# Adding returned rows and last products before gating, and a reordered beginning of the expert stage

## The reference, cut to what matters

```python
for gi in range(N_GROUPS_2):
    hg = jnp.einsum('td,edf->tef', xf, w_gate[gi])
    hu = jnp.einsum('td,edf->tef', xf, w_up[gi])
    act = jax.nn.silu(hg) * hu * comb[:, gi, :, None]   # comb: 0 for experts a token does not use
    out = out + jnp.einsum('tef,efd->td', act, w_down[gi])
...
h = h + gate_f * _hierarchical_moe(xf, ...)
return _rms_norm(h, norm_out_w)
```

## Time and profile before

| | |
|---|---|
| three runs | 1900.52, 1903.16, 1905.74 us, median 1903.16 |
| the profiled execution | 1896.68 us, its span 1894.8 us |
| TensorE busy | 1846.8 us (97%) |
| VectorE busy | 1221.7 us (64%) |
| ScalarE busy | 943.2 us (50%) |
| POOL busy | 104.2 us (5%) |
| mean granted TensorE clock | 0.99 |

### The profile page before, as it was taken

How to read it: one execution, slowest core, us unless ns; L and a number is a source line. 1 busy time by engine, 2 the same in 40 slices (tenths; PEclk the granted TensorE clock), 3 DMA queues, 4 the chain that set the end, 5 groups by cost and what they waited for, 6 DMA issues and landing times.

```text
span 1894.8 us, 24459 instructions
## 1 busy us (share of the span) xinstructions
PE 1846.8 (97%) x9398; PEld 1525.2 (80%) x9398; DVE 1221.7 (64%) x1319; ACT 943.2 (50%) x1035; POOL 104.2 (5%) x118
## 2 busy tenths in 40 slices
PE   8999999999999999999999999989999989999997
PEld 6888998888888888888888888878888778876764
DVE  5566766566654566655555666787645767868677
ACT  5434535444544464544435443564445446767574
POOL 0100000000000000000100000103100050000000
PEclk8999999999999999999999999999999999999999
DMA  6877465777455556554746776535233357979794
GB/s 231 291 254 245 144 200 177 245 249 245 155 194 187 189 169 203 178 178 146 93 80 190 253 250 215 165 116 173 90 112 134 112 213 239 329 248 339 250 336 185
DMA packets 239273, 379.16 MB, mean 200 GB/s; under 512 B 13511, under 2 KB 149069, under 8 KB 239184
## 3 DMA queue, kind: packets, MB, share of 16 engines
q1 hardware_dynamic: 233728, 365.13, 57.3%
q0 software_dynamic: 5456, 12.81, 4.0%
HBM read 372.83 MB, written 10.30 MB: 202 GB/s over the span
## 4 chain that ended last, share of the span: by engine, by line
PE 91%; DVE 5%; ACT 2%; DMA 1%; issue 1%; SPq 0%; POOLq 0%; ACTq 0%; DVEq 0%
PE ps L373 26%; PE ps L375 26%; PE ps L374 26%; PE ps L1056 2%; PE ps L1078 1%; DVE lo L356 1%; PE ps L2756 1%; PE ps L760 1%; PE ps L1066 1%; ACT hi L350 1%; PE ps L1545 1%; PE ps L1034 1%; DVE late L1913 1%; PE ps L1560 0%; PE ps L487 0%
## 5 line engine op out<-in xcount | busy, mean ns | idle before, releaser
L356 DVE TENSOR_TENSOR lo<-raw,hi 128x2048 fp32r<-128x2048 f32 x296 | 678.1, 2296 | 326.2 <-ACT hi L350 325.0
L350 ACT ACTIVATE hi<-raw 128x2048 fp32r<-128x2048 f32 x296 | 565.2, 1915 | 364.5 <-PE ps L375 355.2
L373 PE MATMUL ps<-hi,xT_hi 128*128 128x512 f32 x1376 | 549.8, 400 | 14.4 <-DVE lo L356 7.9
L375 PE MATMUL ps<-hi,xT_lo 128*128 128x512 f32 x1376 | 538.3, 391 | 0.0
L374 PE MATMUL ps<-lo,xT_hi 128*128 128x512 f32 x1376 | 538.1, 391 | 0.0
L373 PEld LDWEIGHTS ps<-hi,xT_hi 128*128 128x128 f32 x1376 | 259.6, 189 | 69.7 <-issue 9.8
L375 PEld LDWEIGHTS ps<-hi,xT_lo 128*128 128x128 f32 x1376 | 259.4, 189 | 56.0
L374 PEld LDWEIGHTS ps<-lo,xT_hi 128*128 128x128 f32 x1376 | 260.0, 189 | 49.6
L373 PE MATMUL ps<-hi,ffn_hhi 128*128 128x512 f32 x352 | 137.8, 391 | 0.0
L375 PE MATMUL ps<-hi,ffn_hlo 128*128 128x512 f32 x352 | 137.1, 389 | 0.0
L374 PE MATMUL ps<-lo,ffn_hhi 128*128 128x512 f32 x352 | 137.0, 389 | 0.0
(11 more groups left out here) (449 smaller groups left out, 2225.5 us busy)
## 6 DMA issues: line engine op xcount, KB each, us to landing
raw<-in_ffn_w_in SPq DMA_DIRECT2D x176, 512.0 KB, 4.6
raw<-in_ffn_w_out SPq DMA_DIRECT2D x88, 512.0 KB, 4.1
raw<-in_attn_w_qkv SPq DMA_DIRECT2D x72, 512.0 KB, 4.6
raw<-in_w_in SPq DMA_DIRECT2D x64, 512.0 KB, 4.4
modraw<-in_mod_w SPq DMA_DIRECT2D x48, 512.0 KB, 6.5
raw<-in_w_gate SPq DMA_DIRECT2D x48, 512.0 KB, 4.5
raw<-in_w_up SPq DMA_DIRECT2D x48, 512.0 KB, 5.8
raw<-in_w_down SPq DMA_DIRECT2D x48, 512.0 KB, 4.4
```

What stands on the lines that cost most here:

```text
L350: nc.scalar.activation(hi[u % SPLIT][:, :], raw[raw_slot(u)][:, :], ACT.Copy).then_inc(S("hi_ready"), 1)
L356: nc.vector.tensor_tensor(lo[u % SPLIT][:, :], raw[raw_slot(u)][:, :], hi[u % SPLIT][:, :].bitcast(F32), ALU.subtract).then_inc(S("lo_read ...
L373: nc.tensor.matmul(dst, w_hi, x_hi, start=start, stop=False, skip_group_check=True)
L375: return nc.tensor.matmul(dst, w_lo, x_hi, start=False, stop=stop, skip_group_check=True)
```

## The change

1. *The end:* both returned rows of both tiles are added first; then, per tile, the products are added out of PSUM, the whole is gated once and added to `h`. `add_gated` for this stage is gone.
2. *The first silus:* the silu table is loaded by a one-column activation after the router's exponentials. A new semaphore `gu_first` is counted when block 0 (block 2) is finished, halfway through the last gate/up unit of position 0 (1), and the first silu waits for that. silu(0) and gate_up(0) come ahead of the gathers of batch 0. Each unit of position 1 waits only for its own pair of gathers.
3. *Routing values:* `info(1)` makes position 1's blocks only, at the old place; the others follow after position 2's second, third and fourth unit. VectorE takes the first part where it took all, and the rest ahead of `inner_lo(3)`; the down units of position 1, and POOL's scatter, wait for the rest.
4. *inner_hi(2) and inner_lo(2)* move ahead of the rounding and the split of position 2's last unit.

```diff
+                           ("weight_rest", 1), ("dest_rest", 1)),
...
-            pool.wait_ge(S("dest_ready"), AT["dest_ready"] + 1)
+            pool.wait_ge(S("dest_rest"), AT["dest_rest"] + 1)
...
             nc.scalar.activation(R("se", 4), R("sx", 4), ACT.Exp).then_inc(S("rt_exp"), 1)
+            nc.scalar.activation(root[:, :], eps[:, :], ACT.Silu)
             round_unit(act, u0 + 3)
...
                 for b in blocks or BLOCKS[n]:
-                    wait_used(act, GUU[n] + 3)
+                    if n < 2 and b == BLOCKS[n][0]:
+                        act.wait_ge(S("gu_first"), n + 1)
+                    else:
+                        wait_used(act, GUU[n] + 3)
...
+            silu(0, 0)
+            silu(0, 1)
             gathered(0, 0)
             gathered(0, 2)
             gathered(0, 4)
             gathered(0, 6)
-            silu(0, 0)
-            silu(0, 1)
             round_unit(act, GUU[1] + 1)
...
+                    if n == 2 and i == 3:
+                        inner_hi(2)
                     round_unit(act, u)
...
-                    if n == 2 and i == 3:
-                        inner_hi(2)
...
-                        dve.wait_ge(S("weight_ready"), AT["weight_ready"] + 1)
+                        ready = "weight_ready" if n == 1 else "weight_rest"
+                        dve.wait_ge(S(ready), AT[ready] + 1)
...
+            def block_info(mm, bs, weight_sem, dest_sem):
+
+                dve.wait_ge(S(mm), AT[mm] + 1)
+                info = ps[:, 5, 0:4 * N_ROUTED].rearrange("p (b q) -> p b q", q=4)[:, bs, :]
+                then(nc.vector.tensor_copy(winfo[:, bs], info[:, :, 3:4].rearrange("p b q -> p (b q)")))
+                nc.vector.tensor_tensor(weight[:, bs], winfo[:, bs], info[:, :, 2:3].rearrange("p b q -> p (b q)"),
+                                        ALU.add).then_inc(S(weight_sem), 1)
+                then(nc.vector.tensor_scalar(dinfo[:, bs], info[:, :, 1:2].rearrange("p b q -> p (b q)"), 1.0, moe_cols[:, 20:21],
+                                             ALU.subtract, ALU.mult))
+                nc.vector.tensor_tensor(dest[:, bs], dinfo[:, bs], info[:, :, 0:1].rearrange("p b q -> p (b q)"),
+                                        ALU.add).then_inc(S(dest_sem), 1)
+
             split_unit(dve, GUU[1])
+            gate_up(0, 0)
+            gate_up(0, 1)
             gathered(0, 1)
             gathered(0, 3)
             gathered(0, 5)
             gathered(0, 7)
-            gate_up(0, 0)
-            gate_up(0, 1)
             split_unit(dve, GUU[1] + 1)
...
+                        block_info("info_mm", slice(0, 2), "weight_ready", "dest_ready")
                         gate_up(1)
...
+                    if n == 2 and i == 3:
+                        inner_lo(2)
                     split_unit(dve, u)
...
-                    if n == 2 and i == 3:
-                        inner_lo(2)
...
                         split_unit(dve, u)
                         if n == 2 and i == 0:
+                            block_info("info_rest", slice(2, N_ROUTED), "weight_rest", "dest_rest")
                             inner_lo(3)
...
             for t in range(TT):
                 dve.wait_ge(S(f"y_loaded{t}"), 32)
-                then(nc.vector.tensor_tensor(y_back[:, t, 0, :], y_back[:, t, 0, :], y_back[:, t, 1, :], ALU.add))
+                nc.vector.tensor_tensor(y_back[:, t, 0, :], y_back[:, t, 0, :], y_back[:, t, 1, :], ALU.add).then_inc(S("y_summed"), 1)
+            for t in range(TT):
+                dve.wait_ge(S("y_summed"), t + 1)
+                wait_acc(dve, DNU[0][1], t)
+                for c in range(2):
+                    y = y_back[:, t, 0, c * 512:c * 512 + 512]
+                    nc.vector.tensor_tensor(y, y, ps[:, 2 * t + c, :], ALU.add).then_inc(S("gated"), 1)
+                dve.wait_ge(S("gated"), 4 + 2 * t + 2)
                 then(nc.vector.tensor_tensor(y_back[:, t, 0, :], y_back[:, t, 0, :], gate_row[:, 1, :], ALU.mult))
-                then(nc.vector.tensor_tensor(h[:, t, :], h[:, t, :], y_back[:, t, 0, :], ALU.add))
+                nc.vector.tensor_tensor(h[:, t, :], h[:, t, :], y_back[:, t, 0, :], ALU.add).then_inc(S("h_ready"), 2)
...
                     pe.wait_ge(S("picked"), 2 * IN_BATCH[m][-1])
+                if m == 1 and f == 0:
+                    pe.wait_ge(S("fill_hi"), 4)
+                    pe.wait_ge(S("fill_lo"), 4)
...
-                    if i == 0:
+                    if n == 1:
+                        pe.wait_ge(S("fill_hi"), i + 1)
+                        pe.wait_ge(S("fill_lo"), i + 1)
+                    elif i == 0:
...
+                    if n < 2 and i == 3 and j == 1:
+                        last.then_inc(S("gu_first"), 1)
...
                     pe.wait_ge(S("e_lo"), BLOCKS[n][-1] + 1)
+                    if n == 1:
+                        pe.wait_ge(S("dest_rest"), AT["dest_rest"] + 1)
...
-            def info():
+            def info(*experts):
...
-                pe.wait_ge(S("picked"), 2 * (N_POS - 1))
-                for n in range(1, N_POS):
+                pe.wait_ge(S("picked"), 2 * experts[-1])
+                if experts[0] > 1:
+                    pe.wait_ge(S("dest_ready"), AT["dest_ready"] + 1)
+                for n in experts:
...
             gate_up_unit(1, 2)
-            info()
+            info(1)
             gate_up_unit(1, 3)
...
                         turn(2 + i)
+                    if n == 2 and i:
+                        info(*((2, 3, 4, 5), (6, 7, 8, 9, 10), range(11, N_POS))[i - 1])
...
-            add_gated(dve, DNU[0][1], 1, ysb_all, 1, (0, 1, 2, 3))
```

More of the change, by code:

```diff
@@ L105, in build @@
             "moe_vector": (("rt_gx", 1), ("rt_sx", 1), ("chosen", 2), ("order_ready", 1), ("rank_read", 1), ("slot_ready", 2), ("xtok_lo", 4),
-                           ("info_vals", 4), ("weight_ready", 1), ("dest_ready", 1)),
+                           ("info_vals", 4), ("weight_ready", 1), ("dest_ready", 1),
+                           ("weight_rest", 1), ("dest_rest", 1)),
             "moe_scalar": (("rt_exp", 2), ("xtok_hi", 4), ("back_ready", 1), ("last_hi", 2)),
-            "moe_tensor": (("rt_mm", 1), ("rank_mm", 1), ("x_turned", 2), ("info_mm", 1), ("last_turned", 1)),
+            "moe_tensor": (("rt_mm", 1), ("rank_mm", 1), ("x_turned", 2), ("info_mm", 1), ("info_rest", 1), ("last_turned", 1)),
         }
@@ L2623, in moe_dve @@
                     if n == 2 and i == 2:
-                        dve.wait_ge(S("info_mm"), AT["info_mm"] + 1)
-                        info = ps[:, 5, 0:4 * N_ROUTED].rearrange("p (b q) -> p b q", q=4)
-                        then(nc.vector.tensor_copy(winfo[:, :], info[:, :, 3:4].rearrange("p b q -> p (b q)")))
-                        nc.vector.tensor_tensor(weight[:, :], winfo[:, :], info[:, :, 2:3].rearrange("p b q -> p (b q)"),
-                                                ALU.add).then_inc(S("weight_ready"), 1)
-                        then(nc.vector.tensor_scalar(dinfo[:, :], info[:, :, 1:2].rearrange("p b q -> p (b q)"), 1.0, moe_cols[:, 20:21],
-                                                     ALU.subtract, ALU.mult))
-                        nc.vector.tensor_tensor(dest[:, :], dinfo[:, :], info[:, :, 0:1].rearrange("p b q -> p (b q)"),
-                                                ALU.add).then_inc(S("dest_ready"), 1)
+                        block_info("info_mm", slice(0, 2), "weight_ready", "dest_ready")
                         gate_up(1)
@@ L2855, in info @@
                                                     slot_info[:, t, RANK[n], :], start=t == 0, stop=t == TT - 1, skip_group_check=True)
-                last.then_inc(S("info_mm"), 1)
+                if experts[-1] in (1, LAST):
+                    last.then_inc(S("info_mm" if experts[-1] == 1 else "info_rest"), 1)
             def last_turn():
```

## The result

| | before | after |
|---|---|---|
| median of 14 runs (lowest to highest) | 1899.74 us (1895.75 to 1905.74) | 1893.72 us (1889.27 to 1897.63) |
| ratio after to before, 95% interval | | 0.9965 (0.9956 to 0.9975) |
| profiled execution: its time, span, granted clock | | 1897.50, 1895.6, 0.988 |

The change makes the kernel 6.0 us faster by the medians, and between 4.8 and 8.4 us by the interval. The kernel before has a median of 1899.74 over its 14 runs, where the three runs that the forecast started from had 1903.16.

The account below looks back on a forecast made before the run. The prediction took TensorE to bound the kernel, with VectorE setting the end. Its terms, -2.3 + 1.7 - 1.5 + 0.2 - 1.4 + 1.6 - 2.5 = -4.2 us, gave 1892.5, plus 6.5 for the median: 1899.0, range 1894.5 to 1902.5.

Parts of the forecast that it names:

- A: TensorE's first wait (2.99 us), before position 1: becomes a 2.5 us wait at fill(1, 3), everything after 2.3 us earlier.
- A': Clock after the new 2.5 us wait: falls to half rate for about 3.4 us, costing +1.7 us.
- a wait of 1.6 is below those that were followed by the lower clock: At the new wait ahead of down_unit(1, 0): 1.6 us is too short to be followed by the lower clock.
- C: Third wait (1.39 us), at turn(3): goes because inner_lo(2) moves ahead of a split; -1.4 us.
- D: New wait ahead of down_unit(1, 0), for VectorE's small operations and inner_lo(3) after the last routing products; +1.6 us.
- B: Second wait (1.56 us), ahead of position 2: goes, with fewer routing products ahead and an earlier silu; -1.5 us.
- E: The kernel's end, set by VectorE's work: 6 full-width operations instead of 8; -2.5 us.
- 1: Rival: the clock does not fall after the new wait at fill(1, 3); -5.9 us, 1897.3; chance 0.19.
- 2: Rival: VectorE's chain isn't what TensorE waits for at fill(1, 3), no new clock fall; -8.3 us, 1894.9; chance 0.08.
- 3: Rival: the new down-unit wait delays VectorE's next split, so TensorE waits again; about -1.9 us, 1901.3; chance 0.10.
- 4: Rival: the lower clock lasts, three stretches of 5 us making the kernel slower; +1.6 us, 1904.8; chance 0.06.
- 5: Rival: the silu table is loaded again, silus stay late; -3.6 us, 1899.6; shares 0.57 with the likeliest case.

Follow-up runs that it names:

- e4: The changed kernel with VectorE's eight permuting operations and the four writing their results moved off the chain ending in the gather, behind position 2's first gathers; ratio to before 0.9945.
- e14: The kernel before, unchanged, profiled once more to look at the clock; no ratio taken.
- e15: The kernel before, unchanged, profiled yet again for the same look at the clock; no ratio taken.
- e2: The changed kernel with the old end put back; ratio to before 0.9977.
- e3: The changed kernel with six unused products of 128 columns put ahead of the wait of fill(1, 3); ratio to before 0.9953.
- e5: The changed kernel with the routing split undone: all 36 routing products at the old place, one group of small operations; ratio to before 0.9978.
- e8: The changed kernel with inner_hi(2) and inner_lo(2) put back behind the rounding and the split; one execution, no ratio.
- e10: The kernel before with the routing split alone added; ratio to before 1.0003.
- e1: The kernel before with the new end alone; ratio to before 0.9984.
- e7: e4 and e5 together: the changed kernel with the permuting moved late and the routing split undone; ratio to before 0.9962.
- e6: The changed kernel with its later routing products in two groups (14, 18) behind position 2's second and third unit, none directly ahead of the down unit; ratio to before 0.9960.
- e9: e4 and e6 together: the changed kernel with late permuting and the later routing products in two groups; ratio to before 0.9929.
- e11: e7 with four products of 128 columns spread among the 36 routing products; ratio to before 0.9949.

## Why the prediction came out short

**The level to start from failed first, and most.** The forecast of 1899.0 took the profiled execution's 1896.68, less 4.2, and added 6.5 because the median of three runs was that much above it. Over 14 runs the median is 3.1 above it, 1899.74; all three lay higher than that. This is 3.4 of the 5.3 us between 1899.0 and 1893.72, and with it put right the same terms give 1895.5. The likelier case (0.61), a difference under 0.3%, did not come either; and the 5.7 us taken for what can be told from none were too much, as the interval is 3.6 us wide. The other 1.8 us are the change's own.

**A, right.** fill(1, 3) starts 21.00 us from the start instead of 23.35: -2.35 for a forecast of -2.3, with a wait of 2.56 for 2.5. e4 shows that the chain through VectorE is what sets it. Against e14 and e15, where fill(1, 3) starts at 24.04, it is 3.0; that belongs to A'.

**A', the clock, is the term of the change that failed.** The new stretch at 0.53 came, as forecast, and costs 1.4 (e2 against after, at R) where +1.7 was put. But I set it against an old one of 3.5 us read from one execution, where its loss was hidden: TensorE still came to fill(1, 3) 0.20 us too early. In two of three executions of before the old stretch is twice as long, and R comes 0.9 later; and the new one stays away in two of eight. From the start to R the means of the executions are 36.56 and 35.11: -1.45 where A + A' gave -0.6. That is 0.85 of the 1.8 us missing, 0.6 of it by the longer old stretch. It is also where "a wait of 1.6 is below those that were followed by the lower clock" goes: 1.47 was followed by it in e3 and e4, and 2.56 was not in e2, nor 2.50 in e5. The very wait of 1.79 that the prediction leans on was followed by it in 7 of 18 executions. So the length of the wait alone doesn't decide, and no threshold lies between the 1.64 and 1.79 of two rows.

**C and D right, B right in size and half wrong in its reason.** From R to D it is 25.87 before and 24.10 after, -1.77 for a forecast of -1.1 (-1.5 + 0.2 - 1.4 + 1.6). The waits of 1.56 and 1.39 are gone and one of 1.47 is there: -1.5. The 0.2 for breaking up the run did not appear: the routing products' groups take 3.05 us in all in after, the one run 3.08 before (1552.42 to 1555.50). A wait that goes may also give back the last product's pipeline: it is listed at 0.39, products in a row come every 0.21, and two waits less and one more leave about 0.2. That last part is argued from rows, not tested. e8 shows C: with part 4 undone the wait at turn(3) is back. For B the prediction shortened TensorE's way to the unit's end from 8.8 to 5.9 us by 32 products fewer, and let the silu start halfway. The silu alone did it: e5 has all 36 products there and no wait, e10 has four and the old wait. So the split of the routing (part 3) brought the wait D and none of B; what speaks for it is only that the lower clock followed the whole run in all three executions with the new beginning.

**E, right.** 12.7 to 10.1, -2.6 for -2.5; from D to S -2.7. e1 alone gives 0.9984. The condition for it, that the second tile's rows are there in time, held.

**Rivals.** 1 (the clock does not fall) happens in two of eight executions of kernels with that wait. 2 is refuted by the wait that names the gather. 3 did not occur: TensorE has no idle time behind the down unit. Nor did 4: with the new beginning no stretch at 0.50 between the start and the last products was longer than 3.5 us. 5 did not occur either, since no table is loaded again ahead of the first silu; true is that the preload does nothing, but the silus are early without it.

**The sum.** By the means: -1.45 - 1.77 - 2.7 = -5.9 us, and the medians say -6.0.

Still open is what makes the clock fall. The run of 36 routing products is followed by it in 3 of 3 executions of the new beginning and in 1 of 4 of the old; but in those three it had not fallen before in the stage, and in those four it had. No run holds the one fixed and changes the other, so nothing here tells which of the two matters.

## What to carry to other kernels

Price a lower clock behind a wait from several executions, since one and the same wait of 2.99 us cost 3.5 or 6.5 us at half rate and one of 2.56 sometimes nothing; count it as a chance and not as a threshold, and look at the next thin place too, where the fall may come instead (e3, e4, e5, e7). Take the level to start from over as many runs as the forecast's range needs: three were 3.4 us off, nearly as much as the change was said to bring. When a wait moves instead of going, look for what can leave the chain that ends it: twelve small VectorE operations taken off it here (e4) brought R another 3.75 us forward in one trace, the clock's part included, where the whole reordering ahead of it had brought 1.45. Keep very thin products in small groups among wide ones, but not directly ahead of the instruction that waits for their result (e6, e9).

## What the runs showed of the hardware

- 36 products of four columns in a row, about 3.1 us in which TensorE is listed as fully busy, were followed by 3.3 us at 0.50, even with four products of 128 columns among them (e5, e7, e11), and in 1 of 4 executions of the old beginning. Groups of up to 18 were not, also where the clock had not fallen before (e9).
- Idle times of 1.47 us were followed by the lower level twice in eight executions (2 of 3 where it had not come shortly before, 0 of 5 where it had), of 1.79 in 7 of 18, of 2.50 to 2.56 for 3.4 us in six of eight, and of 2.99 in all five, for 3.4 or about 6.6 us. That the same code falls differently agrees with the Trainium skill, TensorE: Matmul & The Clock Gate, Part 1, by which the gate's period runs free of the kernel; no run here shows the period itself.
- In an early stage that no kernel changed, the same 10 us held 86 products in one execution, at 1.00, and 49 in another, at 0.50.
